# DeltaNet's last corner products, fresh values and outputs placed between the chunks of the first gate product

## What is computed

```python
def step(s, xs):                       # DeltaNet, one chunk of tokens
    q_c, k_c, u_c, w_c, qk_c, gam_c = xs
    v_new = u_c - jnp.einsum('bhcd,bhde->bhce', w_c, s)
...
    o = (jnp.einsum('bhcd,bhde->bhce', q_c * jnp.exp(gam_c)[..., None], s)
         + jnp.einsum('bhcs,bhse->bhce', qk_c, v_new))
...
def delta_output(o, z, norm_w):
    o = rms_norm(o.transpose(0, 2, 1, 3), norm_w).astype(z.dtype)
    return (o * jax.nn.silu(z.reshape(...))).reshape(b, n, DN_WIDTH)
...
def merge_branches(ya, yb, yc, gates, w_a, w_b, w_c, w_o):
    ga, gb, gc = jnp.split(gates, N_BRANCH, axis=-1)
    m = (jax.nn.sigmoid(ga) * (ya @ w_a) + jax.nn.sigmoid(gb) * (yb @ w_b)
         + jax.nn.sigmoid(gc) * (yc @ w_c))
    return m @ w_o
```

## Time and profile before

| | us |
|---|---|
| median of three runs | 2451.2 (2450.57 to 2452.26) |
| the profiled execution | 2450.02 |
| its span | 2448.2 |
| PE busy in the span | 2373.4 (97%) |
| PE's mean granted clock | 0.994 of full |

### The profile page before, as it was taken

How to read it: one execution, slowest core, us unless ns; L and a number is a source line. 1 busy time by engine, 2 the same in 40 slices (tenths; PEclk the granted TensorE clock), 3 DMA queues, 4 the chain that set the end, 5 groups by cost and what they waited for, 6 DMA issues and landing times.

```text
span 2448.2 us, 37726 instructions
## 1 busy us (share of the span) xinstructions
PE 2373.4 (97%) x15740; PEld 2009.5 (82%) x15740; DVE 1456.4 (59%) x2273; ACT 955.9 (39%) x1556; POOL 133.2 (5%) x170
## 2 busy tenths in 40 slices
PE   6999999999989999999999999999999998999999
PEld 4888888867888888888888888888887688898999
DVE  6877666346768466587654553333354668667654
ACT  4322223356564422242222232322244765544553
POOL 0000000004034000000000000000000203200000
PEclk9999999999999999999999999999999999999999
DMA  7545443201200143335554432222222220054454
GB/s 296 210 181 196 172 155 121 104 35 52 87 19 20 52 155 138 121 120 206 189 194 169 157 112 102 103 86 103 103 94 80 104 87 20 20 186 176 173 191 171
DMA packets 44664, 309.68 MB, mean 126 GB/s; under 512 B 5072, under 2 KB 6224, under 8 KB 7632
## 3 DMA queue, kind: packets, MB, share of 16 engines
q1 hardware_dynamic: 44208, 306.00, 34.0%
q10 hardware_dynamic: 288, 1.27, 0.2%
HBM read 306.20 MB, written 1.05 MB: 126 GB/s over the span
## 4 chain that ended last, share of the span: by engine, by line
PE 88%; DVE 5%; ACT 3%; issue 1%; DMA 1%; SPq 0%; POOL 0%; DVEq 0%; ACTq 0%
PE bank L1583 76%; PE bank L1963 5%; PE bank L1576 2%; PE bank L1876 1%; DMA first_panels<-in_wts 1%; PE bank L1899 1%; DVE u_lo L2295 1%; ACT w_hi L1006 1%; PE bank L1595 1%; PE bank L1885 1%; DVE sq L2287 1%; PE bank L1817 1%; DVE work L2804 0%; DVE w_lo L2247 0%; DMA ring<-in_wts 0%
## 5 line engine op out<-in xcount | busy, mean ns | idle before, releaser
L2247 DVE TENSOR_TENSOR w_lo<-ring,w_hi 128x1024 fp32r<-128x1024 f32 x420 | 511.1, 1224 | 648.3 <-ACT w_hi L1006 643.6
L1583 PE MATMUL bank<-u_hi,w_hi 128*128 128x512 f32 (+1 forms) x2272 | 812.7, 358 | 18.2 <-DVE u_lo L2295 12.6
L1583 PE MATMUL bank<-u_hi,w_lo 128*128 128x512 f32 (+1 forms) x2272 | 800.6, 352 | 0.0
L1583 PE MATMUL bank<-u_lo,w_hi 128*128 128x512 f32 (+1 forms) x2272 | 800.4, 352 | 0.0
L1006 ACT ACTIVATE w_hi<-ring 128x1024 fp32r<-128x1024 f32 x420 | 443.2, 1059 | 820.0 <-PE bank L1583 803.0
L1583 PEld LDWEIGHTS bank<-u_hi,w_hi 128*128 128x128 f32 x2272 | 429.1, 189 | 86.5 <-issue 16.2
L1583 PEld LDWEIGHTS bank<-u_lo,w_hi 128*128 128x128 f32 x2272 | 429.1, 189 | 59.5
L1583 PEld LDWEIGHTS bank<-u_hi,w_lo 128*128 128x128 f32 x2272 | 429.6, 189 | 57.3
L1583 PE MATMUL bank<-hidden_hi,w_hi 128*128 128x512 f32 (+1 forms) x722 | 257.9, 357 | 0.0
L1583 PE MATMUL bank<-hidden_hi,w_lo 128*128 128x512 f32 (+1 forms) x722 | 257.2, 356 | 0.0
L1583 PE MATMUL bank<-hidden_lo,w_hi 128*128 128x512 f32 (+1 forms) x722 | 257.1, 356 | 0.0
(11 more groups left out here) (258 smaller groups left out, 2461.7 us busy)
## 6 DMA issues: line engine op xcount, KB each, us to landing
ring<-in_wts SPq DMA_DIRECT2D x280, 1024.0 KB, 4.8
first_panels<-in_wts SPq DMA_DIRECT2D x8, 1024.0 KB, 6.9
h<-in_x SPq DMA_DIRECT2D x8, 256.0 KB, 4.2
par<-in_par ACTq DMA_DIRECT2D x2, 620.0 KB, 3.8
out<-h SPq DMA_DIRECT2D x8, 128.0 KB, 3.6
cst<-in_cst SPq DMA_DIRECT2D x1, 724.0 KB, 6.4
mod_par<-in_mod SPq DMA_DIRECT2D x1, 96.0 KB, 5.0
cond<-in_c SPq DMA_DIRECT2D x1, 8.0 KB, 1.6
```

Source lines behind the costliest of these rows:

```text
L1583: last = weights.used(pe.matmul(out, lhs[a], rhs[b], start=start and n == 0, stop=stop and n == 2))
L2247: tt(w_lo[:, b % HALVES, :], half_source(n % RING, part), w_hi[:, b % HALVES, :].bitcast(F32), ALU.subtract).then_inc(panel_left[n % RING] ...
```

## The change

The last step's corner products are no longer issued at the end of step 3. They, the fresh values of step 3 and the outputs of step 3 become pieces of a generator that runs within G0: after chunk 2 the corner products of both directions, after chunk 4 the fresh values of both, after chunk 6 the outputs of both. Ahead of G0 stands a wait for `keyed_ready` of both directions, since G0 now writes the bank of `STATE[0]` before `fresh(d, 3)` has waited for it. No instruction is added or removed on another engine, and their order is the same.

```diff
+                    def corners():
+                        for d in range(2):
+                            pe.wait_ge(y_kept[d], (it + 1) * LEVELS)
+                            pe.wait_ge(xt_ready[d], (it + 1) * DEPTHS)
+                            a, b = BEFORE[d], BEHIND[d]
+                            for hd in range(HEADS):
+                                last = mm(ONE[d][a, hd * BLOCK:(hd + 1) * BLOCK], Y[b, d, hd, :],
+                                          heads(T_full[b, d, :])[:, hd, b])
+                            last.then_inc(corner_made[d], 1)
+
+                    if j < 3:
+                        corners()
+
+                def last_step():
+                    yield
+                    corners()
+                    yield
+                    yield
                     for d in range(2):
...
+                        fresh(d, 3)
+                    yield
+                    yield
+                    for d in range(2):
+                        outs(d, 3)
+                    while True:
+                        yield
+
                 for d in range(2):
-                    fresh(d, 3)
-                for d in range(2):
-                    outs(d, 3)
-                std([(l, "gate", 0, 0)], w, u, None, 0)
+                    pe.wait_ge(keyed_ready[d], 3 * (l + 1))
+                std([(l, "gate", 0, 0)], w, u, None, 0, last_step())
```

7 lines of the change are left out of this document (removed).

## The result

The changed kernel takes **2455.2 us** (median of 22 runs, 2452.0 to 2464.2); the kernel before, on the same chips, 2451.6 (median of 22, 2449.8 to 2458.4). The ratio is **1.0016, with an interval of 1.0010 to 1.0022**: about 3.5 us slower by the medians, 3.9 by the ratio, where 0.4 us faster was forecast. It is under 0.2%, but outside the predicted range (up to 2452.9) and on the other side. A second set of 11 runs gave 2456.9 and a ratio of 1.0019 (1.0010 to 1.0027).

What follows compares the result with a forecast made beforehand. PE's list was taken as the bound. First layer -0.81 + 0.35 + 0.03 = -0.43, second -0.43 + 0.46 = +0.03, together -0.4 us: 2451.2 - 0.4 = 2450.8 us. Range 2448.7 to 2452.9 us.

Steps and rivals of the forecast that it cites:

- The bound: Whole kernel: PE's list bounds it, busy 2373.4 of 2448.2 us, and no ring transfer's landing counts.
- The waits taken away: Both layers: gate matmuls fill the waits for `Y` (0.21) and first `V` (0.60), gaining 2 x 0.81 us.
- Changes of shape: Switches between narrow and wide products around gate pieces in both stretches: 0.35 us added a layer, plus 0.03 for restarts.
- The sum: Local terms added: first layer -0.43 us, second layer +0.03, together -0.4 us.
- The squares: First sum in G1: PE waits 0.46 us for ACT's square in the second layer, none in the first.
- What bounds the kernel now: Opening step: PE's list bounds; the two stretches have clock 1.00, so no clock to win; 0.95 us issues nothing.
- The range: Whole kernel time from 2448.7 us (full gain) to 2452.9 us (the tail, plus the highest run's 1.1).
- What would show it: Wrong if: waits at second-layer outputs, first-layer first sum or G2, or shape changes dearer behind a 512-column matmul.
- The chances: Forecast 0.60, whole idle time 0.15, tail 0.20, nothing happens 0.03, late weights or something not seen 0.02.
- late weights or something not seen: At G2: PE waits if work behind the squares slips over 2.5 us more, or anything unforeseen; chance 0.02.
- slower than before: Rival: the chain outputs, L2733, squares, first sum outweighs PE's 0.43 a layer; +0.6, 2451.8 us; chance 0.20.

Runs made afterwards that it cites:

- e1: Kernel before with only the wait for keyed_ready of both directions added ahead of the last fresh values, order unchanged; ratio 1.0000.
- e4: The changed kernel again, unaltered, beside other kernels on the same chip; ratio 1.0019.
- e9: Changed kernel with three first-layer fresh-value products done once more, restoring that stretch to about its old length; ratio 1.0017.
- e13: Repeat of the changed kernel with three first-layer fresh-value products done once more; ratio 1.0014.
- e15: Repeat of the kernel before, old order, with three first-layer output products left out; ratio 1.0012.
- e10: Kernel before, old order, with three first-layer output products left out, stretch 0.67 us shorter; ratio 1.0010.
- e7: Kernel before, old order, with six extra fresh-value products in the first layer, stretch 0.73 us longer; ratio 1.0017.
- e12: Kernel before, old order, with two first-layer fresh-value products done once more, one of each direction; ratio 1.0003.
- e14: New order in the first layer alone, with three fresh-value products there done once more; ratio 1.0010.
- e8: Kernel before with only the last chunk's outputs moved behind G0's first six products, in both layers; ratio 0.9990.
- e3: The whole change in the second layer alone, the first layer as in the kernel before; ratio 1.0009.
- e6: Kernel before, old order, six first-layer output products left out and four second-layer key transposes done twice; ratio 0.9995.

## Why the prediction was wrong

**The bound, right.** PE's list is the bound; no transfer and no other engine became it. The added wait cost nothing (e1).

**The waits taken away, right in kind.** The holes for `Y` and `V` are filled in both layers, and no wait ahead of the outputs came in the second layer, where only 0.07 was in hand.

**Changes of shape, right.** From `beside` to the gate piece and from corner to gate it is 0.20 us from start to start, as forecast: last starts at 798.75 and 801.24. Leaving the gate piece took 0.56 in the first layer and 0.31 in the second (forecast 0.54 and 0.32). What was mis-sized is the corner products themselves. The forecast has their 16 loads one behind the other, 0.058 apart, 0.87 from the first start to the last; the row has 0.82 us less the last load's 0.13, that is 0.69. The single starts in the trace show why: in the first layer each direction's eight are 0.058 apart, but the second direction's begin at 800.83, before the first's last two have (0.29 behind the first's first instead of 0.46). So starts of narrow loads don't strictly follow PE's list one by one. These 0.18 are nearly all of the difference between the 12.66 forecast and 12.45, and between 10.01 and 9.85 (0.69 again in the second layer). Before, the second direction's corner loads waited 0.21 for `Y`, as the prediction read it. The sum said -0.43 for the first layer; it is -0.63.

**The squares, right.** Forecast 0.46 us of waiting at the first sum of the second layer and none in the first. It is the 0.59 by which G1 came earlier, and in the first layer none. Second layer: forecast +0.03, measured 0.00. The 0.16 by which the corner loads were mis-sized there went into this wait.

**The step that failed stands in "What bounds the kernel now": "The clock is 1.00 in both, so no clock is to be won."** With it the clock got no term in the sum. It is true of both stretches, in the trace after too, and it was taken to say that the clock was out of the sum. The clock was only out of the *stretches*. The mean of the profiled execution of before is 0.994, so some 0.6% of the clock was missing somewhere, and the edit moves everything behind it. Of the changed kernel's +3.60 us, the clock's falls carry +2.11 - 1.99 + 1.09 + 2.36 = +3.57, the local gain -0.63, slower products at the full clock (last section) +0.38, and the rest is 0.3 at the ends. In the other trace, e4, the falls carry +6.7. The sum of local terms was right to 0.3 us, and what it left at nothing was nine times its size.

**The range** had no term for it. Its upper end added up late squares and dear shapes. "What would show it" named four local things that would be wrong, and none of them came. The chances had 0.02 for "late weights or something not seen".

**The rival "slower than before"** ended on the right side for a wrong reason. It expected 0.43 of waiting in a layer; the first has none and the second exactly breaks even. Yet the wait is not always without a price: in e9 and e13 the wait for the squares is followed by a fall that costs 4.75 us, and the old order has none with the clock standing alike. That price is the clock's, not the wait's. It is not in the traces of after and e4; whether other executions of the changed kernel paid it is not known.

By the Trainium skill's page "TensorE: Matmul & The Clock Gate", section "What's actually happening", the gate judges recent activity in a free-running window, so that the same kernel pays differently by where it stands in it. The runs here agree as far as they go: one kernel had the fall near 1443 in one execution and not in another (e15, e10), and the place orders the falls of all 18 traces up to 1936 us. None of them shows the window itself.

**What stays open.** The traces show that the falls near 1065, 1442, 1811 and 1892 follow from the place and not from the order, and the means of the clock in the timed executions agree with it. That they make all of the ratio of 1.0016 is not shown. The ratios of the later sets can't show it: e10 and e15 gave 1.0010 and 1.0012, and before against itself 1.0011. It is not known what sets how an execution begins, nor why the 0.38 us near 1940 was in both traces of the changed kernel, on which its long fall near 2022 hangs. The longer fall near 2022 and the one near 2066 are 2.4 of the 3.6 us. Versions without the idle places themselves (the 4.5 us ahead of 2022, the waits ahead of the `beside` loads), where no shift could matter, were not tried.

## What to carry to other kernels

When the bound is PE and its mean granted clock is under 1.00, find the places where it falls before pricing an edit, and give the range a term for their moving: here 1 to 5 us a place, against tenths for the edit itself. An edit worth less than that can't be judged by one time; compare the traces load by load, and pad or shorten the unedited kernel by the same amount to see what the shift alone does. Trace each kernel more than once: how the execution began moved the work against the clock too, by -0.33 to +0.17 us, where the edit moved it by -0.63. What is worth having is an edit that takes away the idle places at which the clock falls.

## What was not expected of the hardware

**The clock's falls move by shifts of tenths of a microsecond, hundreds of microseconds away.** 0.73 us of added products at 800 us changed the stretches at 844, 1070, 1440, 1813, 1892, 2022 and 2069 (e7). 0.21 us changed none (e12). An execution that began 0.23 us earlier against the clock lost the one at 1442 and got two others (e14).

**Products can come 4% slower at a granted clock of 1.00.** In some executions, over stretches of 10 to 180 us, 20 us hold 172 matmuls instead of 179; the record of one is 281 instead of 276 ns long. The last feed-forward block, all of PE busy, before and then e8: the stretch by stretch view, and the groups of 2280 to 2440 us.

```profile
2380.00:2400.00 20.00, 20.00 (x179) 20.00 (x178) 10.16 (x12) 9.43 (x11) 0.00 (x0) 1.00 0.55 198
...
L1583 PE MATMUL bank<-u_hi,w_hi 128*128 128x256 f32 x311 | 85.8, 276 | 0.0
```

```profile
2380.00:2400.00 20.00, 20.00 (x172) 20.00 (x171) 10.29 (x12) 8.66 (x11) 0.00 (x0) 1.00 0.51 179
...
L1583 PE MATMUL bank<-u_hi,w_hi 128*128 128x256 f32 x307 | 86.3, 281 | 0.0
```

That is +7.6 us behind 2132 in e8 and +7.9 in e7, in kernels whose work there is that of before. It may be behind the runs of every kernel that are 5 to 10 us over the others at the same mean clock; those were not traced. It came without a pattern that I could tie to an edit, with one exception that may be chance: the +0.38 us near 1940 to 1950 is such a stretch, and it was in both traces of the changed kernel and in e3, but also in e6, e12 and e13 and in none of the others. Small as it is, it stands ahead of the fall near 2022 and decides its length, by the section on what the traces say together.

**The loads of two groups of narrow products can overlap.** In the changed kernel the second direction's corner loads begin 0.29 us behind the first direction's first one, when two of the first's eight are still to come, at both layers; each group keeps its 0.058 from start to start. Sixteen loads take 0.69 us from the first start to the last, not 0.87.
